# The weight sums of the down projection: from GpSimd to VectorE

## The reference, cut to what matters

```
def mlp(h, w_up, w_down):
    return jnp.square(jax.nn.relu(h @ w_up)) @ w_down
...
xp = xp + mlp(rmsnorm(xp, norm_mlp_g[layer]), w_up[layer], w_down[layer])
xs = xs + mlp(rmsnorm(xs, norm_mlp_g[layer]), w_up[layer], w_down[layer])
```

## Time and profile before

| | |
|---|---|
| median of 3 runs | 1811.37 us (1809.75 to 1812.15) |
| the profiled execution | 1817.1 us, span 1815.5 us |
| granted TensorE clock, mean | 0.983 |
| TensorE busy | 1713.9 us, 94% |
| VectorE busy | 1243.9 us, 69% |
| ScalarE busy | 656.6 us, 36% |
| GpSimd busy | 359.0 us, 20% |

### The profile page before, as it was taken

One profiled execution on the slowest core, in us unless ns is written; L12 is line 12 of the kernel. 1 busy time (PEld: TensorE's weight loads), 2 busy tenths in 40 slices (PEclk: granted clock), 3 DMA queues, 4 the chain that ended last, 5 costly groups with the idle time before them and its releaser, 6 DMA issues.

```text
span 1815.5 us, 37038 instructions
## 1 busy us (share of the span) xinstructions
PE 1713.9 (94%) x14651; PEld 1593.1 (88%) x14651; DVE 1243.9 (69%) x1998; ACT 656.6 (36%) x1331; POOL 359.0 (20%) x340
## 2 busy tenths in 40 slices
PE   7998999999999999889999999999999999899997
PEld 6995766898999989889899898788799998798987
DVE  4336776659687786973588764767747968578695
ACT  4114556433333333431511423632233333233342
POOL 0710000223333140530000000030021503214043
PEclk9999999999999999999999999999999999899998
DMA  8219998237767677453378587431225675322221
GB/s 273 70 59 371 352 359 332 94 121 273 255 232 263 229 270 246 146 178 107 99 222 298 183 279 256 157 117 48 100 75 204 230 269 195 130 80 82 90 71 52
DMA packets 167178, 339.02 MB, mean 187 GB/s; under 512 B 9178, under 2 KB 116500, under 8 KB 165437
## 3 DMA queue, kind: packets, MB, share of 16 engines
q1 hardware_dynamic: 164691, 249.74, 40.7%
q0 software_dynamic: 2240, 87.41, 12.7%
q10 hardware_dynamic: 114, 0.03, 0.0%
HBM read 324.36 MB, written 100.19 MB: 234 GB/s over the span
## 4 chain that ended last, share of the span: by engine, by line
PE 74%; DVE 12%; ACT 4%; DMA 4%; issue 3%; POOL 2%; SPq 1%; DVEq 0%; ACTq 0%; POOLq 0%
PE pp L761 19%; PE pp L1086 16%; PE pp L771 13%; PE pp L724 10%; DVE f_lo L1462 4%; PE pp L836 3%; DMA raw<-in_w_down 1%; PE pp L1035 1%; PE pp L850 1%; ACT f_hi L2192 1%; PE pp L870 1%; PE pp L1193 1%; PE pp L1240 1%; DMA raw<-in_w_up 1%; PE pp L1218 1%
## 5 line engine op out<-in xcount | busy, mean ns | idle before, releaser
L771 PE MATMUL pp<-bf_hi,f_hi 128*128 128x288 f32 x896 | 273.8, 306 | 48.1 <-DVE x L1479 26.7
L771 PE MATMUL pp<-bf_lo,f_hi 128*128 128x288 f32 x896 | 270.7, 302 | 0.0
L771 PE MATMUL pp<-bf_hi,f_lo 128*128 128x288 f32 x896 | 269.8, 301 | 0.0
L771 PEld LDWEIGHTS pp<-bf_hi,f_hi 128*128 128x128 f32 x896 | 174.2, 194 | 55.1 <-DVE f_lo L1462 41.7
L761 PE MATMUL pp<-a_hi,whi 128*128 128x288 f32 x1024 | 219.8, 296 | 0.7 <-DVE zbuf L1495 0.7
L761 PE MATMUL pp<-a_lo,whi 128*128 128x288 f32 x1024 | 219.3, 296 | 0.0
L761 PE MATMUL pp<-a_hi,wlo 128*128 128x288 f32 x1024 | 219.2, 296 | 0.0
L2128 ACT ACTIVATE whi<-raw 128x1024 fp32r<-128x1024 f32 x83 | 88.0, 1060 | 329.7 <-PE pp L1086 195.5
L1086 PE MATMUL pp<-a_hi,whi 128*128 128x288 f32 x768 | 177.6, 313 | 0.3 <-DVE proj L1792 0.3
L771 PEld LDWEIGHTS pp<-bf_lo,f_hi 128*128 128x128 f32 x896 | 174.1, 194 | 0.0
L771 PEld LDWEIGHTS pp<-bf_hi,f_lo 128*128 128x128 f32 x896 | 174.0, 194 | 0.0
(11 more groups left out here) (335 smaller groups left out, 3353.5 us busy)
## 6 DMA issues: line engine op xcount, KB each, us to landing
kvring<-in_cache_b_kv SPq DMA_DIRECT2D x128, 512.0 KB, 5.7
out_new_d_sample<-in_cache_d_kv POOLq DMA_DIRECT2D x32, 2040.0 KB, 8.4
raw<-in_w_up SPq DMA_DIRECT2D x32, 1024.0 KB, 5.4
raw<-in_w_down SPq DMA_DIRECT2D x32, 1024.0 KB, 4.9
kring<-in_cache_d_kv SPq DMA_DIRECT2D x104, 256.0 KB, 3.2
vring<-in_cache_d_kv SPq DMA_DIRECT2D x104, 256.0 KB, 5.1
raw<-in_w_in_cd SPq DMA_DIRECT2D x24, 1024.0 KB, 5.2
out_new_d_sample<-in_cache_d_kv POOLq DMA_DIRECT2D x8, 2016.0 KB, 8.5
```

Source lines behind the costliest of these rows:

```text
L771: last = pe.matmul(product_bank(m), w[s_][:, k, :], b[:, f, k, :], start=(k == 0 and n == 0 and p in (0, 1, 3)), stop=(k == 3 and n == 2), ...
```

## The change

The function `sums` moves from GpSimd's part to VectorE's, with the same waits and the same four additions. VectorE makes group 0 after up tile 5, group 1 after the low parts 4 to 6 and before it reads product 1, groups 2 and 3 after it has read products 8 and 15. GpSimd's `chunk` keeps the copies alone.

```diff
--- before.py
+++ after.py
@@ -1452,6 +1452,23 @@
                                              op1=ALU.subtract).then_inc(a_ready, 1)
                 return post
 
+            def sums(L, t0, c, i):
+
+                done = c * 16 + (64 * L + 4 * i)
+                dve.wait_ge(raw_loaded[i % 2], c * 64 + 16 * (LOADS[t0] + 2 + i // 2 + 1))
+                if i >= 2:
+                    dve.wait_ge(wlo_ready, in_chunk(t0, c, 8 + 7 * (i - 1)))
+                elif not isinstance(c, int) or c:
+                    dve.wait_ge(wlo_ready, in_chunk(t0, c, 8 + 7 * (i + 3) - CHUNK))
+                w, s_ = raw_q[i % 2], w_sum[i % 2]
+                a11, a12, a21, a22 = w[:, :, 0, 0, :], w[:, :, 1, 0, :], w[:, :, 0, 1, :], w[:, :, 1, 1, :]
+                dve.tensor_tensor(s_[2], a11, a21, ALU.subtract).then_inc(w_sums, 1)
+                dve.tensor_tensor(s_[0], a21, a22, ALU.add).then_inc(w_sums, 1)
+                dve.wait_ge(w_sums, done + 2)
+                dve.tensor_tensor(s_[1], s_[0], a11, ALU.subtract).then_inc(w_sums, 1)
+                dve.wait_ge(w_sums, done + 3)
+                dve.tensor_tensor(s_[3], a12, s_[1], ALU.subtract).then_inc(w_sums, 1)
+
             def mlp(L, t0):
 
                 bb = B_BASE[L]
@@ -1542,10 +1559,15 @@
 
                     for u in range(8):
                         up_tile(c, u, first and u == 0)
+                        if u == 5:
+                            sums(L, t0, c, 0)
                     for m in (4, 5, 6):
                         form_lo(m, c)
+                    sums(L, t0, c, 1)
                     for m in range(1, DOWN):
                         read(m, c)
+                        if m in (8, 15):
+                            sums(L, t0, c, m // 7 + 1)
                         if m in FORM_AFTER:
                             form_lo(FORM_AFTER[m], c)
                         if m == 24 and not (last and L == 1):
@@ -2685,37 +2707,16 @@
 
             QROWS = (WIN[2] - TS) // 4
 
-            def sums(L, t0, c, i):
-
-                done = c * 16 + (64 * L + 4 * i)
-                pool.wait_ge(raw_loaded[i % 2], c * 64 + 16 * (LOADS[t0] + 2 + i // 2 + 1))
-                if i >= 2:
-                    pool.wait_ge(wlo_ready, in_chunk(t0, c, 8 + 7 * (i - 1)))
-                elif not isinstance(c, int) or c:
-                    pool.wait_ge(wlo_ready, in_chunk(t0, c, 8 + 7 * (i + 3) - CHUNK))
-                w, s_ = raw_q[i % 2], w_sum[i % 2]
-                a11, a12, a21, a22 = w[:, :, 0, 0, :], w[:, :, 1, 0, :], w[:, :, 0, 1, :], w[:, :, 1, 1, :]
-                pool.tensor_tensor(s_[2], a11, a21, ALU.subtract).then_inc(w_sums, 1)
-                pool.tensor_tensor(s_[0], a21, a22, ALU.add).then_inc(w_sums, 1)
-                pool.wait_ge(w_sums, done + 2)
-                pool.tensor_tensor(s_[1], s_[0], a11, ALU.subtract).then_inc(w_sums, 1)
-                pool.wait_ge(w_sums, done + 3)
-                pool.tensor_tensor(s_[3], a12, s_[1], ALU.subtract).then_inc(w_sums, 1)
-
             def chunk(L, t0, c, beside_up, beside_down):
 
                 for u in (0, 2, 4, 6):
                     if beside_up:
                         pool.wait_ge(tile_done, in_chunk(t0, c, u + 1))
                         beside_up(u // 2)
-                    if u >= 4:
-                        sums(L, t0, c, u // 2 - 2)
                 for m in (0, 7, 14, 21):
                     if beside_down:
                         pool.wait_ge(tile_done, in_chunk(t0, c, 8 + m + 1))
                         beside_down(m // 7)
-                    if m < 14:
-                        sums(L, t0, c, m // 7 + 2)
 
             def widest(b):
```

## The result

The kernel after takes **1847.02 us** (median of 4 runs, 1845.35 to 1849.15), the kernel before on the same chip 1810.64 (4 runs): ratio 1.0201, 95% interval 1.0183 to 1.0218. The forecast was 1840.6 with a range of 1822 to 1858. The sign and the places were as forecast, several terms of the sum were not. The profiled execution after took 1849.15 us (span 1847.6); that of before took 1817.1 (span 1815.5).

A forecast was written before the change was run, and what follows sets the result against it. TensorE was taken as the bound nearly everywhere. Five plain chunks (+21.0), two last chunks (+4.5) and the narrow copies' chunk (+3.7) made +29.2 us on the median of 1811.37: 1840.6 us, range 1822 to 1858.

The forecast's parts named there:

- Price of a group: A group of four additions on VectorE takes 2.7 us, between 2.4 and 3.7, judged from the low part.
- Product 4 starts 0.8 us later: In a plain chunk, groups 0 and 1 on VectorE delay the start of product 4 by 0.8 us.
- The stop of 5.6 us: TensorE finishes products 1 to 3 early, then stands still 5.6 us in one piece before product 4.
- The clock, +1.2 taken: Behind the long stop before product 4, TensorE runs at half speed: +1.2 us a plain chunk, between 0 and 3.
- Products 11 and 18, 1.1 each: Groups 2 and 3 on VectorE each stop TensorE 1.1 us, before products 11 and 18 of a chunk.
- the signs named: Stop of 5 to 6 us before product 4, half clock behind; 1.1 before products 11 and 18; 105 us per chunk.
- The last chunks, +4.5 for both: Last chunk of each layer: +2.2 and +2.3 us, as earlier stops of 2.37, 1.22 and 1.06 us go.
- The narrow copies, +3.7: Second layer's second chunk: two 21.9 us cache copies hold loads of groups 2 and 3; it ends 3.7 us later.
- Same DMA engines: Rival: second narrow copy queues behind the first; second layer's second chunk +18.8 us, not +3.7; total 1856; chance 0.20.
- Slow additions: Rival: additions on VectorE take 3.7 us a group, +8.2 us a plain chunk; total 1871 us; chance 0.06.
- Faster: Rival: additions on VectorE cost 0.37 us each; a plain chunk gains 1.8 us; total 1793 us; chance 0.06.
- No change: Rival: sums fit into VectorE's idle time, clock stays up, relief pays for the rest; total 1811 us; chance 0.06.

The follow-up runs named there:

- Experiment 4: Kernel after, with additions of groups 1 to 3 one or two at a time between readings and group 0 behind up tile 4: 1795.28 us, ratio 0.9878.
- Experiment 6: Kernel after, with seven plain fp32 multiplications read by nobody put on TensorE ahead of product 4: 1834.31 us, ratio 1.0120.
- Experiment 1: Kernel after, with groups 2 and 3 back on GpSimd, so only groups 0 and 1 on VectorE: 1825.64 us, ratio 1.0045.
- Experiment 9: Kernel after, with GpSimd's additions of squares in the last chunks 8 columns wide in place of 576: 1836.03 us, ratio 1.0117.
- experiment 7: Kernel after, with the second narrow cache copy issued behind product 14 in place of product 7: 1851.80 us, ratio 1.0226.
- 8: The kernel of Experiment 4, with the two narrow cache copies cut into eight pieces of 32 rows: 1779.71 us, ratio 0.9824.
- 10: Kernel before (sums on GpSimd), with only the two narrow cache copies cut into eight pieces of 32 rows: 1799.49 us, ratio 0.9923.
- experiment 3: Kernel after, with group 1 behind reading 2 in place of ahead of reading 1: 1839.91 us, ratio 1.0122.

## Why the prediction was right, and where its sum was not

**Price of a group: right.** 2.66 us measured, 2.7 taken. The nearest row, the low part, was the right row. The Trainium skill (GPSIMD Engine Reference, "Engine selection") sends elementwise work to VectorE; the trace agrees per instruction (0.69 us against 1.62), and the kernel got slower. Experiment 4 shows both at once: the same additions gain 1.2% in other places.

**Product 4 starts 0.8 us later: it starts 0.4 earlier.** The mean hides the chunks: +0.5 (11.40 to 11.89 us) in chunk 1 of the first layer, on which the sum was made, and −1.7 in a chunk where before needed 13.58 us. The stretch of before varies from 11.2 to 13.6 us with GpSimd's timing, and I took one chunk for all.

**The stop of 5.6 us: 4.26.** I let TensorE run through products 1 to 3 without a wait. In chunk 1 product 1 starts 0.3 us later than that, and product 2, which waits for the reading of product 0 behind up tile 7's work, another 0.6 (a stop of 0.43); so products 1 to 3 end about a microsecond later than I had them, and product 4 starts 0.3 us sooner than forecast. The end of the stop is VectorE's, so the later beginning cost nothing.

**The clock, +1.2 taken: 1.9.** This term is mis-sized. I carried over the 3 us of half speed of the earlier trace rows; behind the stop it was 4.6 us in chunk 1, of which half is lost, at most 2.3; over the same 4.6 us two of the five plain chunks show 0.63 in place of 0.50. Experiment 6, which keeps the clock up and changes no wait, gives 1.9 (12.48 against 14.42 us). It lies inside the bounds of 0 to 3.

**Products 11 and 18, 1.1 each: right**, 1.06 in the rows, and 1.2 in the stretch (12.48 against 11.28 us from product 11 to 18). Experiment 1 takes these stops away.

Together a plain chunk is +3.99 against +4.2, with errors of −1.2 and +1.0 that nearly cancel. That the sum came out better than its parts is luck. Of the signs named, the long stop came at 4.3 us and not at 5 to 6, and chunk follows chunk after 106 us, not 105; the others came.

**The last chunks, +4.5 for both: +8.9.** This is the step that failed. I wrote that GpSimd's sums of squares "no longer queue behind weight sums", and that the stops of the earlier trace rows therefore go. They no longer queue; just for that they run at once, beside the sums that were moved, at more than the double price, as the earlier trace rows show for such a meeting. The rows for it were on the table: I used the contention where it was relieved and did not ask who else GpSimd would meet. Experiment 9 prices it: without the squares the last chunks are 0.3 and 0.2 us below those of before, so the meeting costs 5.8 + 3.6 = 9.4 us.

**The narrow copies, +3.7: +4.9.** The chain was right: product 11 was forecast for 30.2 us behind product 0 and came at 30.3, product 18 for 49.4 and came at 50.4, since the second load came 25.7 us behind its copy and not 24.5. That the loads are held by these copies is shown by experiment 7 (move the copy, and another load is held) and by 8 and 10 (cut it, and none is).

**The rivals.** *Same DMA engines* fell: the load for group 2 came 24.4 us after the first copy, without waiting for the second, and the chunk grew by 4.9 and not 18.8. Experiment 4 shows it more plainly, for there the copies overlap: the second was issued 13.3 us behind the first (1515.93 and 1529.21) and landed 22.3 us later, at 1551.6; queued behind the first on the same engines it would have ended at about 1515.9 + 2 × 21.9 = 1559.7, an estimate from the earlier trace rows. That the second copy takes other engines than the first, as the Trainium skill (DMA: Bandwidth & Descriptors, "Why a DMA increments its semaphore by 16 and not by 1") would have it, agrees with that; no row tells which engine a packet took. *Slow additions* fell: 0.69 us each. *Faster* fell in this order of work only; its price per addition (0.37 us) was wrong, and experiment 4 was faster by another way. *No change* needed TensorE to have more in hand than two products; the stops of 1.06 us show that it has not.

The sum comes out at +33.8 us in the product stretches against +29.2, and 4.4 of the missing 4.6 are the last chunks; the plain chunks (−1.0) and the narrow copies (+1.2) cancel. The medians lie 36.4 us apart, the spans of the profiled executions 32.1: that of before was slower than the median of its 4 runs by 6.5, that of after by 2.1.

## What to carry to other kernels

Moving work to the faster engine is decided by the turn it takes there: four additions in a block ahead of a reading stopped TensorE by 1 us and more, the same four spread between readings by some half a microsecond at most in a plain chunk, and the two kernels differ by 3%. When an engine is relieved, ask what on it now starts earlier and beside whom; busy totals will not show it, the rows of one stage will. And a stop of TensorE has two prices, the wait and the half clock behind it: a filler that changes no wait tells them apart.

## What the runs showed of the hardware that was not expected

The half clock does not follow from a stop's length alone. Behind stops of 4.26 to 4.28 us it came in every plain chunk, behind 1.60 us in none of experiment 4's. In between it went either way: the same two stops of 1.61 and 1.79 us (experiment 3) left 1.00 in three plain chunks and 0.66 and 0.63 in two, and stops of 2.3 and 2.9 us in the second layer's last chunk left 1.00 in the kernel after and 0.63 and 0.61 in experiment 6. What decides there stays open; no run was made for it.

A copy of four rows of 480 KB each takes 21.9 us, and a load issued behind it from SyncE lands 24 to 26 us after the copy's issue (experiments 4, 6 and 7 and the kernels before and after); cut into eight of 480 KB and 32 rows, the copies land in 4.2 us each and hold nothing that TensorE waits for. The form of a copy, not its bytes, was worth 0.8% of this kernel.

Where these operations of VectorE meet GpSimd's, the two do not share: one stands still. In the last chunk GpSimd's addition runs from 781.08 for 1.66 us, to 782.74; VectorE's, begun at 781.51, ends at 783.29, so 0.55 us behind it, less than the 0.69 it needs alone. All ten operations that met one in the kernel after end 0.55 us behind an instruction of GpSimd, whatever their start, and so does the addition beside GpSimd's copy in experiment 9 (784.76 against 784.21). The additions, low parts and the finishing operation, with two inputs in SBUF, suffer (0.69 to 1.78, 0.81 to 1.98); the readings, with one input in a bank, take 449 ns on average in the kernel before and 451 after, when 32 groups of GpSimd's sums have gone; in the kernel before 64 of the 224 run beside an instruction of GpSimd, and these take 447 on average and 456 at most. The Trainium skill (SBUF — State Buffer, "Who interferes with whom") says that the two engines contend over a shared pair of ports alone, which is locked as a whole, and that a VectorE instruction with two SBUF inputs contends with a GpSimd instruction that reads SBUF while one with a single SBUF input does not. These rows agree.
